# Chains that split their own input: the first two weight blocks taken abreast, one chunk of columns at a time

## What is computed

```python
proj = jnp.einsum('bsd,dn->bsn', x, w_in)          # q, k, v, gates and so on of both branches
qkv = jax.nn.silu(_causal_conv(qkv_b, conv_w))     # 3072 features
y = (jax.nn.sigmoid(gate_a) * jnp.einsum('bsc,cd->bsd', ha, w_branch_a)
     + jax.nn.sigmoid(gate_b) * jnp.einsum('bsc,cd->bsd', hb, w_branch_b))
gt, up = jnp.split(jnp.einsum('bsd,df->bsf', x, w_ffn_up), [D_FF_2], axis=-1)
ffn = jnp.einsum('bsf,fd->bsd', jax.nn.silu(gt) * up, w_ffn_down)
```

## Time and profile before

| | us |
|---|---|
| median of three runs | 4377.89 (4377.66 to 4385.02) |
| the profiled execution | 4381.01 |
| its span, first to last instruction | 4379.2 |
| TensorE matmuls busy (PE) | 3860.3, 88% of the span |
| TensorE weight loads busy (PEld) | 3165.7, 72% |
| VectorE (DVE) | 1900.5, 43% |
| ScalarE (ACT) | 1234.8, 28% |
| GpSimd (POOL) | 238.9, 5% |
| mean granted clock of TensorE | 0.925 of full |

### The profile page before, as it was taken

One profiled execution on the slowest core, in us unless ns is written; L12 is line 12 of the kernel. 1 busy time (PEld: TensorE's weight loads), 2 busy tenths in 40 slices (PEclk: granted clock), 3 DMA queues, 4 the chain that ended last, 5 costly groups with the idle time before them and its releaser, 6 DMA issues. The chain is left out here.

```text
span 4379.2 us, 52698 instructions
## 1 busy us (share of the span) xinstructions
PE 3860.3 (88%) x20305; PEld 3165.7 (72%) x20305; DVE 1900.5 (43%) x2569; ACT 1234.8 (28%) x1839; POOL 238.9 (5%) x300
## 2 busy tenths in 40 slices
PE   7787999989999587998889989958699888898997
PEld 6656999966888364785887778846387588686886
DVE  3365524335433324375444443332436544544333
ACT  2243212234222322323323232223222323323222
POOL 0000000000000000001330000000100033000000
PEclk9888999979999698997999999988799899998999
DMA  2101222211222111220002122212022100122222
GB/s 106 49 9 39 91 93 87 87 33 58 100 96 96 33 58 39 78 95 20 0 0 85 70 93 95 90 46 77 0 96 91 44 1 0 52 100 70 91 94 83
DMA packets 52158, 279.08 MB, mean 64 GB/s; under 512 B 12081, under 2 KB 15161, under 8 KB 23773
## 3 DMA queue, kind: packets, MB, share of 16 engines
q1 hardware_dynamic: 51986, 276.75, 18.6%
HBM read 274.43 MB, written 2.27 MB: 63 GB/s over the span
## 5 line engine op out<-in xcount | busy, mean ns | idle before, releaser
L317 PE MATMUL ps<-xs,ffn_w 128*128 128x512 f32 x2112 | 484.4, 392 | 29.5 <-DVE xs L561 29.5
L317 PEld LDWEIGHTS ps<-xs,ffn_w 128*128 128x128 f32 x2112 | 399.7, 189 | 114.6 <-issue 31.1
L317 PE MATMUL ps<-u,mlp_w 128*128 128x264 f32 (+1 forms) x2880 | 456.2, 321 | 14.8 <-DVE mlp_w L555 10.0
L317 PEld LDWEIGHTS ps<-u,mlp_w 128*128 128x128 f32 x2880 | 417.2, 190 | 53.4 <-issue 15.5
L317 PE MATMUL ps<-hn,mlp_w 128*128 128x264 f32 (+1 forms) x2304 | 363.7, 320 | 0.0
L317 PEld LDWEIGHTS ps<-hn,mlp_w 128*128 128x128 f32 x2304 | 332.4, 188 | 30.4 <-issue 0.5
L317 PE MATMUL ps<-xs,cv_w 128*128 128x512 f32 x1152 | 268.2, 394 | 13.5 <-DVE xs L561 9.8
L317 PEld LDWEIGHTS ps<-xs,cv_w 128*128 128x128 f32 x1152 | 217.5, 190 | 64.2 <-issue 17.7
L317 PE MATMUL ps<-ff,ffn_w 128*128 128x512 f32 x1056 | 240.0, 389 | 0.0
L355 ACT CAST ffn_w<-raw 128x2048 fp32r<-128x2048 f32 (+1 forms) x74 | 124.0, 1676 | 383.2 <-PE ps L317 343.2
L317 PEld LDWEIGHTS ps<-ff,ffn_w 128*128 128x128 f32 x1056 | 198.2, 188 | 41.2
(11 more groups left out here) (422 smaller groups left out, 5497.3 us busy)
## 6 DMA issues: line engine op xcount, KB each, us to landing
raw<-in_w_ffn_up SPq DMA_DIRECT2D x44, 1024.0 KB, 4.9
raw<-in_w_up SPq DMA_DIRECT2D x32, 1024.0 KB, 4.8
raw<-in_w_down SPq DMA_DIRECT2D x32, 1024.0 KB, 4.8
raw<-in_w_conv SPq DMA_DIRECT2D x24, 1024.0 KB, 4.9
raw<-in_w_ffn_down SPq DMA_DIRECT2D x32, 704.0 KB, 4.0
raw<-in_w_mqk SPq DMA_DIRECT2D x10, 1024.0 KB, 5.7
raw<-in_w_mo SPq DMA_DIRECT2D x8, 1024.0 KB, 4.9
mv_raw<-in_w_mv SPq DMA_DIRECT2D x16, 512.0 KB, 6.2
```

The costliest lines, as they stand in the source:

```text
L317: ins = nc.tensor.matmul(bank(u)[:, h, :], w[:, s, wp, k * g.bw + j * P:k * g.bw + (j + 1) * P], g.xs[:, xp, k, h * n:(h + 1) * n], start= ...
```

## The change

For a chain with `whole` and without a root to apply, `abreast` is 2. ACT and DVE make the quarter pieces of blocks 0 and 1 together, piece by piece, with two input chunks behind each pair of pieces. TensorE runs blocks 0 and 1 in one go (`two_blocks`): for each chunk it does the three passes of all four tiles, and all four are finished with the last chunk. The step that prepared block 1 as a whole falls away on ACT and DVE, and the loop over the other blocks starts at block 2.

```diff
--- before.py
+++ after.py
@@ -233,6 +233,7 @@
             if g.inv is not None:
                 g.inv_ready = (previous.s["summed"], previous.tiles) if i else (x_summed, KC) if squares is not None else None
         last = gemms[-1]
+        abreast = 2 if whole is not None and gemms[0].inv is None else 1
 
         def tile_no(g, t, after_stat):
             return g.t0 + t + (g.extra if after_stat else 0)
@@ -320,6 +321,28 @@
                                         stop=(k == g.kc - 1 and e == 2))
                         ins.then_inc(filled, 1)
 
+                def two_blocks(g):
+
+                    cuts = [g.kc * q // 4 for q in range(4)]
+                    for k in range(g.kc):
+                        if k in cuts[:3]:
+                            pe.wait_ge(piece_low, 2 * cuts.index(k) + 2)
+                        if k == cuts[3]:
+                            pe.wait_ge(g.s["low_done"], 2)
+                        pe.wait_ge(x_low, k + 1)
+                        for b in range(2):
+                            for j in range(g.tpb):
+                                u = slot_of(g, b, j)
+                                if k == 0:
+                                    pe.wait_ge(freed, tile_no(g, b * g.tpb + j, True) + 1)
+                                for e, (wp, xp) in enumerate(PASSES):
+                                    for h in range(halves):
+                                        ins = nc.tensor.matmul(
+                                            bank(u)[:, h, :], w[:, b, wp, k * g.bw + j * P:k * g.bw + (j + 1) * P],
+                                            g.xs[:, xp, k, h * n:(h + 1) * n], start=(k == 0 and e == 0), stop=(k == g.kc - 1 and e == 2))
+                                if k == g.kc - 1:
+                                    ins.then_inc(filled, 1)
+
                 def sum_squares(g, i):
                     u = (g.t0 + g.tpb) % TILES
                     pe.wait_ge(freed, g.t0 + g.tpb + 1)
@@ -330,10 +353,15 @@
                     ins.then_inc(filled, 1)
 
                 for i, g in enumerate(gemms):
-                    step(g, 0, 0, i)
+                    done = 1
+                    if i == 0 and abreast == 2:
+                        two_blocks(g)
+                        done = 2
+                    else:
+                        step(g, 0, 0, i)
                     if g.inv is not None:
                         sum_squares(g, i)
-                    rolled(pe, g.n_blocks - 1, g.unroll, lambda b, pos: step(g, b + 1, pos + 1))
+                    rolled(pe, g.n_blocks - done, g.unroll, lambda b, pos: step(g, b + done, pos + done))
 
             @block.scalar
             def _(act):
@@ -406,10 +434,12 @@
 
                 g = gemms[0]
                 cuts = [g.kc * q // 4 for q in range(5)]
-                act.wait_ge(ws.first_in[0], 16 * (before + 1))
+                for b in range(abreast):
+                    act.wait_ge(ws.first_in[b], 16 * (before + 1))
                 for q in range(4):
                     part = slice(cuts[q] * g.bw, cuts[q + 1] * g.bw)
-                    nc.scalar.copy(w[:, 0, 0, part], ws.raw[:, 0, part]).then_inc(piece_high if q < 3 else g.s["high_done"], 1)
+                    for b in range(abreast):
+                        nc.scalar.copy(w[:, b, 0, part], ws.raw[:, b, part]).then_inc(piece_high if q < 3 else g.s["high_done"], 1)
                     for c in range(cuts[q], cuts[q + 1]) if whole is not None else ():
                         if gain is None:
                             nc.scalar.copy(g.xs[:, 0, c, :], whole[:, c, :]).then_inc(x_high, 1)
@@ -425,7 +455,8 @@
                         act.sem_inc(g.s["half_done"], 2)
 
                     def step(b, pos):
-                        high(g, b + 1, pos + 1)
+                        if not (i == 0 and abreast == 2 and isinstance(b, int) and b == 0):
+                            high(g, b + 1, pos + 1)
                         if g.inv is not None and isinstance(b, int) and b == 0:
                             root(g)
                         evacuate(g, b, pos)
@@ -551,9 +582,10 @@
                 cuts = [g.kc * q // 4 for q in range(5)]
                 for q in range(4):
                     part = slice(cuts[q] * g.bw, cuts[q + 1] * g.bw)
-                    dve.wait_ge(*((piece_high, q + 1) if q < 3 else (g.s["high_done"], 1)))
-                    nc.vector.tensor_tensor(w[:, 0, 1, part], ws.raw[:, 0, part], w[:, 0, 0, part].bitcast(F32),
-                                            ALU.subtract).then_inc(piece_low if q < 3 else g.s["low_done"], 1)
+                    for b in range(abreast):
+                        dve.wait_ge(*((piece_high, abreast * q + b + 1) if q < 3 else (g.s["high_done"], b + 1)))
+                        nc.vector.tensor_tensor(w[:, b, 1, part], ws.raw[:, b, part], w[:, b, 0, part].bitcast(F32),
+                                                ALU.subtract).then_inc(piece_low if q < 3 else g.s["low_done"], 1)
                     for c in range(cuts[q], cuts[q + 1]) if whole is not None else ():
                         dve.wait_ge(x_high, c + 1)
                         high_part = g.xs[:, 0, c, :].bitcast(F32)
@@ -577,7 +609,8 @@
                         nc.vector.memset(g.total, 0.0).then_inc(g.s["result"], 1)
 
                     def step(b, pos):
-                        low(g, b + 1, pos + 1)
+                        if not (i == 0 and abreast == 2 and isinstance(b, int) and b == 0):
+                            low(g, b + 1, pos + 1)
                         if g.inv is not None and isinstance(b, int) and b == 0:
                             invert(g)
                         evacuate(g, b, pos)
```

## The result

The changed kernel takes 4460.19 us (4445.74 to 4464.85, four runs), the kernel before 4377.77: a ratio of 1.0179, 95% interval 1.0153 to 1.0204. Timed again with five runs it gave 4458.02 and 1.0184 (1.0171 to 1.0197). So it is slower by 80 to 82 us by the medians (78 and 81 by the ratios); 4449 was forecast, 71 slower, in a range that holds the measured time.

The account below looks back on a forecast made before the run. TensorE, busy 88% of the span, was taken to bound the kernel. Late starts, third-block stalls, clock losses and cv's delay added 71.2 us to the median 4377.9, giving 4449 us, range up to 4464 from 4432.

Parts of the forecast that it names:

- Nothing is taken away: At chain starts TensorE waits for no chunk inside the first tile, nor for block 1, so the change gains 0.
- A later start: Ahead of each chain's first chunk DVE does a second piece of weights, costing 0.6 us per chain.
- No third block: Block 2 is prepared only after tile 1 ends; TensorE stalls 3.7 (mqk), 3.3 (ffn), 4.9 (branch_b), 5.6 us (mlp1).
- cv pays its ring: In cv, low parts from the DVE and ACT loop come 11.56 us apart; its whole delay costs 13.2 us per chain.
- cv's own stall: In cv, TensorE's wait for the third block alone, worked out as 10.0 us per chain.
- The clock: Half clock behind the stall in each of seven chains outside cv costs 1.6 us; bounds 0 and 2.3.
- The row that was to show that shorter gaps do it too: A profile stretch at 0.52 clock after 2.93 us idle, taken to show that short gaps also lower TensorE's clock.
- The sum: Over the nine chains: mqk 11.8, ffn 11.0, branch_b 14.2, mlp1 7.8, cv 26.4; together 71.2 us slower.
- the starved first tile: Rival: each chain's first tile is fed too slowly and the change fills it, 12 us faster, 4366; chance 2%.
- no fall of the clock: Rival: third-block stalls come as worked out, but TensorE's clock does not drop behind them, 4438; chance 15%.
- cv's stall alone: Rival: each cv chain pays only its 10.0 us stall and 0.6 late start, total 4444; chance 10%.
- The two rules of the Trainium skill: Breaking up ACT/DVE steps should gain, but no bubble exists; four groups ending together give up evacuation overlap, no price given.

Follow-up runs that it names:

- prep_only: Changed kernel's joint preparation of blocks 0 and 1, but TensorE runs block 0, then block 1, tile by tile as before: 4399.41 us, ratio 1.0048.
- half: Changed kernel with TensorE chunk by chunk over all four tiles only for chunks 0 to 3, then finishing each tile in turn: 4398.96 us, ratio 1.0037.
- table: Changed kernel plus one tiny ACT function between the weight pieces in branch_b and ffn, so its table loads early: 4454.58 us, ratio 1.0180.
- not_cv: Changed kernel, but the two cv chains keep their old order, one block at a time: 4434.91 us, ratio 1.0122.
- fill: Changed kernel plus 14 to 38 matmuls that nobody reads behind each chain's first 96, keeping TensorE busy in the gap: 4443.44 us, ratio 1.0154.
- warm: Kernel before plus one unread float32 matmul of 512 columns ahead of the first wait of each of the nine chains: 4377.69 us, ratio 0.9996.

## Why the prediction was right, step by step

**Nothing is taken away.** Right. Neither chunks nor block 1 had been waited for, and no term of gain shows in any run; the 96 matmuls take 23.0 to 24.7 us from the first start to the last in the changed kernel's profiles, 23.2 to 24.1 before. Yet the reason behind it hung on the pace of 0.9 us per chunk; prep_only shows that at 1.2 us the first tile does starve.

**A later start, 0.6 per chain.** Right: 61.2 + 5.4 against 56.3 + 4.8 is 5.5 in nine places.

**No third block.** Right in mechanism, shown by half. In size mqk (3.5 idle, 3.7 with the part of the cadence that the row counts as busy) and mlp1 (5.4 against 5.6) came out as worked out. By the same count branch_b took 6.05 against 4.9 and ffn 4.5 against 3.3, 1.2 longer, because the table load had moved behind the wait for tile 0. I had taken the loads' place in the kernel before, ahead of tile 0's end, as given, though the cast that they stood behind was one that the change takes away. The run called table shows that the load is the whole of it. That is 4 x 1.2 = 5 us of the miss.

**cv pays its ring.** Right in mechanism: 26.4 was forecast, 27 is the difference to not_cv, 26.0 and 27.3 stand in the traces, and the low parts keep their pace of 11.56. That the size fits so well is in part luck, for two terms were off and cancel. cv's own stall is 9.1 to 9.3, not 10.0: the first two tiles' taps take 3.0 each, not the 3.34 of the loop (first taps at 1887.06 and 1890.08 in the profile after). That makes 12.5 of the 13.2, and 12.3 is what the one chain shows whose first 96 matmuls took 23.0 us. In the other three they took 24.3 to 24.4, with half clock for 5.7 to 5.9 us at the start in place of 3.4, and the ring hands this 1.3 on to the end.

**The clock.** Every gap was followed by half clock, as taken, but a gap costs 1.9 to 2.1 and not 1.6 us (fill). The mis-sized term is the length: half clock lasted 2.8 to 6.2 us behind the gaps, 4.1 on average, and I had taken cv's start, 3.4, as typical. The kernel before had shown that it is not, at the starts of branch_b and ffn:

```profile
2321.90:2326.00 4.10, 4.10 (x10) 0.50 0.00 0
2529.40:2534.20 4.80, 4.80 (x12) 0.50 0.00 0
```

2.3 stood as the upper bound. The row that was to show that shorter gaps do it too says less than I made of it: in the 4.00 us to 2896 TensorE was busy for only 1.10, so more than the one gap of 2.93 stood ahead of the slow stretch. The gap of 2.99 in half bears the statement out.

**The sum.** Late starts outside cv 7 x 0.6 = 4.2; third block 32.8 idle and 7 x 0.17 of cadence, 34.0; clock 13.5; cv 27.3. Together 79, against 79.7 in the nine chains of the second profile and 80.6 by the ratio; without the clock, 38.2 against 38.8 in fill's seven. As forecast these were 4.2, 29.4, 11.2 and 26.4. Of the rivals, the starved first tile is out for the kernel before, whose row is unbroken; no fall of the clock (4438) is out by fill; cv's stall alone (10.6 a chain) is out by the traces.

**The two rules of the Trainium skill.** On the first, in Perfetto Trace Analysis, Optimizing Scalar/DVE Operations, that breaking up ACT and DVE instructions which cause bubbles may let work finish sooner: no run here shows a gain from it, as there was no bubble, and prep_only, which breaks up block 1's cast and keeps the old order of the matmuls, lost 21 us. The second, in the Trainium skill's Perfetto Trace Analysis, Optimizing Tensor Performance, that one group's evacuation should overlap the next group's matmuls, is what half bears out: finishing the four tiles in turn, with the same matmuls, took 64 of the 80 us back (1.0184 to 1.0037).

## What to carry to other kernels

Before filling a wait, look whether the engine waits inside the stretch or only ahead of it, and whether it is slow by its clock. When tiles are taken abreast, all of them end together: ask when the first buffer comes free, and what evacuation, table load and preparation then stand in a row with nothing over them. Finish the tiles in turn as soon as the shortage of input is over. Here even that stayed 16 us behind one block at a time (half), for there was no shortage to cure. And in a ring of two engines (cast, subtract, evacuate) a delay at its head is paid to its end, while a cast moved ahead of an evacuation can open it.

## What the runs showed of the hardware

Gaps of 3.0 to 9.1 us in otherwise dense stretches (half's 2.99, the nine of the changed kernel) were each followed by half clock, for 2.8 us at the shortest and 6.2 at the longest, and keeping TensorE at unread matmuls avoided it in all nine places (fill). One matmul of 1.1 to 2 us ahead of a chain (warm) did not reliably. The same stretch of an untouched stage ran once at 0.59 and once at 0.50 of the clock in two executions of one kernel, and by the start of mlp1 the two were 4.7 us apart. A table load of ACT took 1.28 us and ran 1.7 us ahead of its function, under TensorE's work, in one kernel, and behind the function's wait in the other.
